# Sparse-attention gates, compressed scores and compress products with the small operand held in TensorE and the wide one streamed

## The reference

```python
def compress(t, pos, w1, w2):              # once for keys, once for values; 4 groups of width 64
    ch = t.reshape(B, S // 16, 16, G, DH)
    blocks = jnp.concatenate([ch[:, :-1], ch[:, 1:]], axis=2) + pos[:, None, :]
    flat = ...reshape(B, 15, G, 32 * 64)
    return jax.nn.silu(flat @ w1) @ w2     # w1: 2048 x 256, w2: 256 x 64
...
q = rms_norm(q); k_c = rms_norm(compress(k_c, ...)); v_c = compress(v_c, ...)
k_s, k_w = rms_norm(k_s), rms_norm(k_w)
gates = jax.nn.sigmoid(g)                  # g: 48 columns of the input projection
s = jnp.einsum('bqgnd,bcgd->bgnqc', q, k_c) * scale     # 16 heads x 256 queries x 15 keys
p_c = masked_softmax(s, ...)               # times gate 0, then with v_c
```

## Time and profile before

| what | us |
|---|---|
| runs: median, lowest, highest | 1793.6, 1793.3, 1796.4 |
| profiled execution, span from first to last instruction | 1790.9 |
| TensorE busy, over that span (83%) | 1489.2 |
| VectorE busy (44%) | 787.4 |
| start of `nkv` to start of the attention loop (1010.6 to 1118.5) | 107.9 |
| of it `cmp` (1036.1 to 1050.5) | 14.4 |
| of it `ngate` (1097.7 to 1105.6) | 7.9 |
| of it `cmp_s` (1105.6 to 1118.5) | 12.9 |

### The profile page before, as it was taken

One profiled execution on the slowest core, in us unless ns is written; L12 is line 12 of the kernel. 1 busy time (PEld: TensorE's weight loads), 2 busy tenths in 40 slices (PEclk: granted clock), 3 DMA queues, 4 the chain that ended last, 5 costly groups with the idle time before them and its releaser, 6 DMA issues. The chain is left out here.

```text
span 1790.9 us, 26831 instructions
## 1 busy us (share of the span) xinstructions
PE 1489.2 (83%) x11250; PEld 1165.0 (65%) x11250; DVE 787.4 (44%) x1166; ACT 578.9 (32%) x834; POOL 33.8 (2%) x39
## 2 busy tenths in 40 slices
PE   6999997889966565565755799988999989889999
PEld 3788975578942121121211698448999989779999
DVE  4352445476641000000000756565655475865553
ACT  4332134575221101010100531464333354743332
POOL 2000020000000000000000000000000000100000
PEclk8999998999968787887687897899999999899999
DMA  9554456642729999999999552862545534335540
GB/s 397 236 228 174 163 212 237 229 145 98 279 99 419 429 427 427 426 429 427 427 429 425 213 189 94 321 244 94 184 177 183 187 141 166 141 126 182 187 165 24
DMA packets 46749, 437.94 MB, mean 245 GB/s; under 512 B 5200, under 2 KB 5456, under 8 KB 6064
## 3 DMA queue, kind: packets, MB, share of 16 engines
q1 hardware_dynamic: 45792, 430.99, 61.0%
q0 software_dynamic: 560, 5.01, 0.7%
q10 hardware_dynamic: 288, 0.32, 0.1%
HBM read 435.25 MB, written 1.05 MB: 244 GB/s over the span
## 5 line engine op out<-in xcount | busy, mean ns | idle before, releaser
L677 PE MATMUL bank<-H_r,ring_r 128*128 128x256 f32 x3488 | 511.9, 288 | 18.5 <-DVE H_r L1611 18.5
L677 PEld LDWEIGHTS bank<-H_r,ring_r 128*128 128x128 f32 x3488 | 466.6, 196 | 24.3 <-issue 22.6
L677 PE MATMUL bank<-arena_r,ring_r 128*128 128x256 f32 x2776 | 407.0, 291 | 38.1 <-DVE ring_r L1634 26.8
L1634 DVE TENSOR_TENSOR ring_r<-ring,ring_r 128x2048 fp32r<-128x2048 f32 x136 | 319.1, 2348 | 223.3 <-ACT ring_r L1324 223.0
L677 PEld LDWEIGHTS bank<-arena_r,ring_r 128*128 128x128 f32 x2776 | 377.2, 197 | 54.4 <-issue 26.6
L1324 ACT ACTIVATE ring_r<-ring 128x2048 fp32r<-128x2048 f32 x136 | 259.5, 1909 | 221.1 <-PE bank L677 176.8
L1013 PE MATMUL bank<-ring,arena 128*32 128x512 f32 x1024 | 171.6, 807 | 126.2 <-DMA ring<-in_w 124.3
L1013 PEld LDWEIGHTS bank<-ring,arena 128*32 128x32 f32 x1024 | 34.5, 129 | 251.7 <-DMA ring<-in_w 146.7
L1895 DVE TENSOR_TENSOR arena<-arena,bank 64x512 f32<-64x512 f32 x16 | 11.1, 691 | 280.8 <-ACT arena L1426 280.8
L1426 ACT ACTIVATE arena<-bank 64x512 f32<-64x512 f32 x16 | 9.4, 589 | 368.8 <-PE bank L1013 368.8
L1040 PE MATMUL bank<-ring,arena 128*32 128x256 f32 x1024 | 85.8, 495 | 26.6 <-DMA ring<-in_w 21.4
(11 more groups left out here) (245 smaller groups left out, 1253.4 us busy)
## 6 DMA issues: line engine op xcount, KB each, us to landing
ring<-in_w SPq DMA_DIRECT2D x216, 1024.0 KB, 4.9
ring<-in_w SPq DMA_DIRECT2D x96, 2048.0 KB, 25.6
ring<-in_bias POOLq DMA_DIRECT2D x1, 2048.0 KB, 10.5
consts<-in_consts POOLq DMA_DIRECT2D x1, 1439.0 KB, 9.8
X<-in_x SPq DMA_DIRECT2D x1, 1024.0 KB, 5.5
arena<-in_ctx SPq DMA_DIRECT2D x1, 1024.0 KB, 7.9
arena<-in_decay POOLq DMA_DIRECT2D x1, 1024.0 KB, 11.6
out_t<-X SPq DMA_DIRECT2D x4, 256.0 KB, 2.0
```

The source lines that it names most:

```text
L677: i = nc.tensor.matmul(o, lhsT, rhs, start=start, stop=stop, skip_group_check=grouped)
L1634: v.tensor_tensor(r(lo), lo, r(hi), ALU.subtract).then_inc(lo_ready, 1)
```

## The change

The three products exchange their operands. `cmp` handles keys and values together: for each of the 16 slices of w1 the 60 (with overrun 64) columns of `flat` are stationary, the keys' in array columns 0 to 63, the values' in 64 to 127, and 256 columns of w1 are streamed. `ngate` holds 128 columns of the gate weights (48 wanted ones and their neighbours) and streams 256 tokens. `cmp_s` holds 64 rows x 32 compressed keys, in four column tiles and two row halves, and streams 512 query columns. Each result now lies turned, so ScalarE or VectorE writes it to SBUF (`hid_tok`, `gate_rows`, `cmp_raw`), TensorE transposes it (`cmp_turn`, `ngate_turn`, `cmp_st`) and it is copied or used from there. `nsa_parts` splits 592 instead of 384 gate columns on VectorE, and the mask additions become eight of half the width per half.

The order changes too. `cmp_k` and `cmp_v` move behind `nqk` 3, `nnorm` 2 moves ahead of `nqk` 3, `nnorm` 6 ahead of `nv` 1, and one pair of `mod` chunks stands between `cmp_s` and `ngate_turn`, ahead of the loop.

```diff
@@ -129,11 +129,14 @@
 
-    s += [("nkv", 0), ("nkv", 1), ("nqk", 0), ("nqk", 1), ("cmp", 0, 0), ("cmp", 0, 1), ("cmp", 1, 0),
-          ("cmp", 1, 1), ("cmp_k",), ("cmp_v",), ("nnorm", 0), ("nnorm", 1)]
-    s += [("nqk", 2), ("nqk", 3), ("nnorm", 2), ("nqk", 4), ("nnorm", 3), ("nqk", 5), ("nnorm", 4), ("nsa_parts",),
-          ("nv", 0), ("nnorm", 5), ("nv", 1), ("nnorm", 6), ("ngate",), ("cmp_s",)]
+    s += [("nkv", 0), ("nkv", 1), ("nqk", 0), ("nqk", 1), ("cmp", 0, 0), ("cmp", 1, 0), ("cmp", 0, 1),
+          ("cmp", 1, 1), ("nnorm", 0), ("nnorm", 1)]
+    s += [("nqk", 2), ("cmp_turn",), ("nnorm", 2), ("nqk", 3), ("cmp_k",), ("cmp_v",), ("nqk", 4), ("nnorm", 3),
+          ("nqk", 5), ("nnorm", 4), ("nsa_parts",), ("nv", 0), ("nnorm", 5), ("nnorm", 6), ("nv", 1), ("ngate",),
+          ("cmp_s",)]
     fill += blocks(LAST_BLOCKS, MOD_BLOCKS)
+    take(2)
+    s += [("ngate_turn",), ("cmp_st",)]
     for i in range(PAIRS + LAG + 1):
         take(2)
...
@@ -323,11 +326,18 @@
+            add(("cmp_s", 0), "act")
+            add(("cmp_s", 1), "dve")
+        elif k == "cmp_st":
-                add(("cmp_s", half), "dve")
+                add(("cmp_st", half), "dve")
+        elif k == "cmp_turn":
+            add(x, "dve")
+        elif k == "ngate_turn":
+            add(x, "act")
-            if x[2] == 1:
-                add(("cmp", x[1]), "act")
+            if x[1:] == (1, 1):
+                add(("cmp",), "act")
...
@@ -1071,58 +1083,78 @@
             def step_ngate():
                 pe.wait_ge(wide_split, 1)
                 b = begin(("ngate",))
+                for k in range(KT):
+
+                    n = slice(64 * k + 16, 64 * k + 16 + P)
+                    mm3(b[:, 0:T], (wide_hi[:, n], wide_lo[:, n]), h3(k), k == 0, k == KT - 1,
+                        job_done if k == KT - 1 else None)
+
+            def step_ngate_turn():
+                in_sbuf(("ngate",))
+                b = begin(("ngate_turn",))
                 for t in range(2):
-                    for k in range(KT):
-                        mm3(b[:, t * 48:t * 48 + 48], [x[:, t * P:(t + 1) * P] for x in h3(k)],
-                            (wide_hi[:, k, :], wide_lo[:, k, :]), k == 0, k == KT - 1,
-                            job_done if t == 1 and k == KT - 1 else None)
+                    tr(b[:, t * 48:t * 48 + 48], gate_rows[:, t * P:(t + 1) * P], job_done if t else None, rows=48)
 
             cmp_bank = [None]
 
             def step_cmp(kv, part):
-                ck = chunk(("cmp", kv, part))
+                if kv == 0:
+                    return
+
+                ck = [chunk(("cmp", i, part)) for i in range(2)]
                 if part == 0:
-                    pe.wait_ge(flat_ready, kv + 1)
-                    cmp_bank[0] = begin(("cmp", kv))
+                    pe.wait_ge(flat_ready, 2)
+                    cmp_bank[0] = begin(("cmp",))
+                for j in range(8):
+                    for i in range(2):
+                        at = 7200 + 960 * i + 60 * (8 * part + j)
+                        mm(cmp_bank[0][64 * i:64 * i + 64, 0:T], arena[:, at:at + 64], ck[i][:, j, :],
+                           part == 0 and j == 0, part == 1 and j == 7,
+                           job_done if part == 1 and j == 7 and i else None, grouped=True)
+                owed[0] += 2
+
+            def step_cmp_turn():
+                in_sbuf(("cmp",))
+                b = begin(("cmp_turn",))
                 for ht in range(2):
-                    for j in range(8):
-                        f = flat[kv][:, 8 * part + j, :, :]
-
-                        mm(cmp_bank[0][:, ht * 60:ht * 60 + 60], ck[:, j, ht * P:(ht + 1) * P], f,
-                           part == 0 and ht == 0 and j == 0, part == 1 and j == 7,
-                           job_done if part == 1 and ht == 1 and j == 7 else None, grouped=True)
-                owed[0] += 1
+                    tr(b[:, ht * P:(ht + 1) * P], hid_tok[:, ht * P:(ht + 1) * P], job_done if ht else None)
 
             def step_cmp_k():
-                in_sbuf(("cmp", 0))
+                in_sbuf(("cmp_turn",))
...
             def step_cmp_s():
                 pe.wait_ge(n_normed, 7)
+                b = [begin(("cmp_s", half)) for half in range(2)]
+                for j in range(4):
+                    for half in range(2):
+                        rows = slice(64 * half, 64 * half + 64)
+
+                        mm(b[half][32 * j:32 * j + 32, :], qk[rows, 3072:3104], qk[rows, 1024 + 512 * j:1536 + 512 * j],
+                           True, True, job_done if j == 3 else None)
+
+            def step_cmp_st():
                 for half in range(2):
-                    b = begin(("cmp_s", half))
-                    rows = slice(64 * half, 64 * half + 64)
-                    for qt in range(2):
-                        for qi in range(8):
-                            gp, at = qi // 4, (qt * 8 + qi) * N_CMP
-                            mm(b[:, at:at + N_CMP], qk[rows, 1024 + qi * T + qt * P:1024 + qi * T + (qt + 1) * P],
-                               qk[rows, 3072 + gp * N_CMP:3072 + (gp + 1) * N_CMP], True, True,
-                               job_done if qt == 1 and qi == 7 else None)
+                    in_sbuf(("cmp_s", half))
+                    b = begin(("cmp_st", half))
+                    for i in range(4):
+
+                        at = i // 2 * T + i % 2 * P
+                        tr(b[:, i * P:(i + 1) * P], cmp_raw[half][:, at:at + P], job_done if i == 3 else None)
...
@@ -1445,24 +1478,27 @@
             def step_ngate():
-                takes(f(n_gate.rearrange("p t n -> p (t n)"), job(("ngate",))[:, 0:96], ACT.Sigmoid), ("ngate",))
+                takes(f(gate_rows, job(("ngate",))[0:48, 0:T], ACT.Sigmoid), ("ngate",))
+
+            def step_ngate_turn():
+                takes(f(n_gate.rearrange("p t n -> p (t n)"), job(("ngate_turn",))[:, 0:96], ACT.Copy), ("ngate_turn",))
 
             def step_cmp(kv, part):
-                if part == 1:
-                    takes(f(hid_c[:, kv, :, :], job(("cmp", kv))[:, 0:120].rearrange("p (a b) -> p a b", a=2),
-                            ACT.Silu), ("cmp", kv))
+                if (kv, part) == (1, 1):
+                    takes(f(hid_tok, job(("cmp",))[:, 0:T], ACT.Silu), ("cmp",))
 
             def step_cmp_s():
+                takes(f(cmp_raw[0], job(("cmp_s", 0))[:, :], ACT.Copy), ("cmp_s", 0))
+
+            def step_cmp_st():
                 act.wait_ge(cmp_arg, 1)
                 v = cmp_p.rearrange("p t h c -> p (t h c)")
                 f(v, v, ACT.Exp).then_inc(cmp_exp, 1)
...
@@ -1923,13 +1960,19 @@
+                if kv:
+
+                    i = v.memset(arena[:, 9120:9124], 0.0)
                 i.then_inc(flat_ready, 1)
+
+            def step_cmp_turn():
+                takes(v.tensor_copy(hid_c, job(("cmp_turn",))[:, 0:T].rearrange("p (a b) -> p a b", a=2)), ("cmp_turn",))
...
@@ -1946,30 +1989,41 @@
             def step_nsa_parts():
                 v.tensor_copy(r(ident_1), ident)
                 v.tensor_copy(r(causal_1), const("causal")).then_inc(mask_ready, 1)
-                link(v.tensor_copy(r(wide_hi), wide[:, :, 16:64]))
-                v.tensor_tensor(r(wide_lo), wide[:, :, 16:64], r(wide_hi), ALU.subtract).then_inc(wide_split, 1)
+                flat_wide = wide.rearrange("p k n -> p (k n)")
+                for n, src in ((slice(0, 512), flat_wide), (slice(512, 592), flat_wide[:, 0:80])):
+                    link(v.tensor_copy(r(wide_hi[:, n]), src))
+                    i = v.tensor_tensor(r(wide_lo[:, n]), src, r(wide_hi[:, n]), ALU.subtract)
+                i.then_inc(wide_split, 1)
...
             def step_cmp_k():
-                takes(v.tensor_copy(qk[:, 3072:3102], job(("cmp_k",))[:, 0:30]), ("cmp_k",))
+                keys = qk[:, 3072:3104].rearrange("p (g c) -> p g c", g=2)
+                v.memset(keys[:, :, N_CMP], 0.0)
+                takes(v.tensor_copy(keys[:, :, 0:N_CMP], job(("cmp_k",))[:, 0:30].rearrange("p (g c) -> p g c", g=2)),
+                      ("cmp_k",))
             def step_cmp_s():
+                takes(v.tensor_copy(cmp_raw[1], job(("cmp_s", 1))[:, :]), ("cmp_s", 1))
+
+            def step_cmp_st():
                 add = const("cmp_add").rearrange("p (t c) -> p t c", t=2)
                 keep = const("cmp_keep").rearrange("p (t c) -> p t c", t=2)
                 for half in range(2):
-                    ps = job(("cmp_s", half))[:, 0:240].rearrange("p (t q c) -> p t q c", t=2, q=8)
-                            i = v.tensor_tensor(cmp_p[:, t, h:h + 4, :], ps[:, t, 4 * gp:4 * gp + 4, :],
-                                                over(add[:, t, :], 4), ALU.add)
-                    takes(i, ("cmp_s", half))
-                taken(("cmp_s", 1))
+                            for i in range(2):
+                                o = v.tensor_tensor(cmp_p[:, t, h + 2 * i:h + 2 * i + 2, :],
```

(28 more changed lines are left out.)

2 lines of the change are left out of this document (1 added, 1 removed).

## The result

The changed kernel takes 1779.27 us in the median of five runs (1777.8 to 1781.1), the kernel before beside it 1793.29; the ratio is 0.9922 with a 95% interval of [0.9905, 0.9939], 14.0 us faster. The forecast was 1784.2 in a range of 1779.0 to 1790.5: right in sign, and within the range by 0.3 us. It had forecast 9.4 us, two thirds of the gain.

The account below looks back on a forecast made before the run. TensorE bounds up to `nnorm` 0 and from `nnorm` 6 to the loop, VectorE's chain between. Path 11.2 - clock 4.7 + loop start 2.3 + loop 0.6 = 9.4 us: 1793.6 to 1784.2, range 1779.0 to 1790.5.

Parts of the forecast that it names:

- The bound: Before the loop: TensorE bounds up to `nnorm` 0 and from `nnorm` 6 to the loop, VectorE's chain between them.
- TensorE's saving: Busy time in `cmp`, `ngate` and `cmp_s` falls by 7.4 + 4.7 + 11.8, less 2.9 for transposes: 21 us.
- the transposes: New TensorE steps, 8 instructions read as 4 transposes: `cmp_turn` 0.5, `ngate_turn` 0.4, `cmp_st` 2.0 us.
- The path: From `cmp` to the loop's first maximum: that maximum starts at 1113.2 instead of 1124.37, 11.2 us earlier.
- so 5 of the 7.4 us of `cmp` go here: At TensorE's 7.1 us wait before `nnorm` 2: 5 us of the saving in `cmp` are lost there.
- The clock: Behind the new waits before `nnorm` 2 and 6: half clock costs 2.35 us each, 4.7 us together.
- The loop's part: At the loop: 2.3 us from a VectorE wait that goes, net 0.6 from the moved `mod` pair.
- Rival 1: Behind the two new waits: the clock costs nothing, so 1779.5 us; chance 0.12.
- Rival 2: In `cmp`: weight loads are exposed after all, 64 loads make 4.0 us, so 1788.2 us; chance 0.05.
- Rival 3: In the loop: VectorE and ScalarE pace it and take back 2.3 and 0.6 us, so 1787.1; chance 0.09.
- Rival 5: In `ngate`: wide gate weights cost as much as the narrow product, 4.7 us missing, so 1788.9; chance 0.02.
- Rival 4: In `cmp` and `cmp_s`: no tiles overlap, 16.6 us more, 1800.8; chance 0.10 (0.06 in full, 0.04 one form alone).

Follow-up runs that it names:

- recip_half: Changed kernel with the reciprocal of `nnorm` 0 and 1 over half the columns, 1.6 us less on VectorE twice; median 1775.8 us, ratio to before 0.9907.
- the three orders: Changed kernel with `nnorm` 2, `nnorm` 6 or both put back in their places before the change; medians 1776.5, 1774.1 and 1770.7 us.
- both_late: Changed kernel with `nnorm` 2 back behind `nqk` 3 and `nnorm` 6 back behind `nv` 1; median 1770.7 us, ratio to before 0.9876.
- warm: Changed kernel with dummy matmuls, eight ahead of the wait for `nnorm` 2 and four ahead of `nnorm` 6; median 1778.3 us, ratio to before 0.9919.
- cmp_serial: Changed kernel with the values' half of `cmp` sent to the keys' array columns and left out of later steps; median 1787.2 us, ratio to before 0.9970.

## Why the prediction came out as it did

**The bound** (what bounds the kernel now): right. The two bounds, TensorE to `nnorm` 0 and from `nnorm` 6, VectorE between, are what recip_half and the three orders show. TensorE's saving was put at 21 us and measured at 21.5, but that match is partly luck. The 21 left out the half clock on both sides. Without the moved steps' half clock the busy time falls by 27.4 us (both_late): the transposes were dearer in the forecast than in the trace, and the slow rows behind the old narrow products, 3.64 instead of 1.92 us for the first `mod` pair, went too.

**The path**: right in its times, wrong in one reason. Counted from the start of `cmp` (1036.12 before, 1036.02 after), `nnorm` 0 was to be scaled at 8.1 us and was at 8.2. The wait before `nnorm` 2 was put at 7.1 us and is 7.71, that before `nnorm` 6 at 4.1 and is 4.35. The step that failed is "so 5 of the 7.4 us of `cmp` go here". The wait belongs to the moved `nnorm` 2 alone. With `cmp` old it was 7.92, with `cmp` in turn 7.71, with the order old 1.96. The forecast time does not hang on that sentence, since the sum went by the starts and not by it. The text had the true cause one sentence earlier ("before, `nqk` 3 covered this") and booked the loss on the wrong part; whoever followed it would have judged the fast `cmp` nearly worthless and kept the order.

**The terms that were mis-sized.** Against warm, where the clock costs nothing, A should be 88.25 - 11.2 = 77.05 and is 74.9: 2.2 us too pessimistic. The largest part, 1.1 us, is the transposes. I read 8 instructions as 4 transposes, as for an fp32 matmul; the ten of `ngate_turn` and `cmp_st` show that a transpose is one instruction, and both steps take 1.27 us to the next start instead of 2.4. `nv` 1 takes 5.84 us from start to start in warm, where the forecast had a row's length of 6.31; `nnorm` 6 starts 0.4 earlier than forecast, and the gates were 2.9 for 3.2. From the last transpose to the first maximum it was 0.3 us more than the 6.2 forecast. The clock was put at 4.7 us and costs 3.35 (warm). The loop's part was put at 2.3 + 0.6 = 2.9, and the loop (B less A) went from 89.8 to 86.6, 3.3 in this pair of executions. So 2.2 + 1.35 + 0.4 = 3.9 us are added to the 9.4 forecast, which is the 13.3 of B. One more term was too large: 2.7 us were put outside the span, a median less the span of one execution, while the time of the changed kernel's profiled execution is 2.1 above its own span. That the measured time still lies in the range rests on the low end, which was set by a rival's price for the clock and not by these terms.

**The rivals.** Rival 1 (no cost of the clock) is refuted by the rows of warm, though the time (1779.3) lies where it had it (1779.5). That is chance: the clock costs 3.35 us, and it was the other terms that were too dear. Rival 2 (exposed loads) is refuted by 7.13 us for 64 loads and matmuls, 0.25 over the 6.88 of streaming alone that the prediction had. The Trainium skill ("TensorE: Matmul & The Clock Gate", section "Part 3: Packing small matmuls") has a load overlap with running matmuls only where the row group differs. These 64 loads share all their row groups, and the 7.13 us speak against it for this form. That section of the Trainium skill also names a second case, a load that goes to a background weight buffer, which would fit; no run here shows which buffer a load uses. Rival 3 did not happen: the loop became 3.3 us shorter. Rival 5 is refuted by the 24 instructions of `ngate` in 2.96 us. Rival 4 was priced well, as cmp_serial shows (14.03 us for 13.8), and did not happen: the 64*32 form, which no row of before had, takes 1.09 us for the 1.1 assumed.

## What to carry to other kernels

In this kernel the products whose free side was narrow paid for their weight loads. Hold the narrow operand instead, put two or four such products side by side in the array's columns, and turn the result back: here this was worth 21 us of 178 (both_late), and in `cmp` nearly all of it came from the tiles side by side. Then look at the order apart from the operands. A step that closes a chain over several engines wants independent work between its link on the other engine and its own matmul; moved right behind its source it cost 7.8 us here (10.3 in the old kernel), which only runs of the order alone could show. And where waits remain, move work there from a stage that has too much of it.
